# Layer 1 of a four-layer kernel: values stationary, merge and gate by features, three token blocks open in its output projection

## The chip, the cores and the metric

The kernel runs on one core of one Trainium2 chip. The metric is the device time of one execution in microseconds (us). The kernel before takes 2743.85 us, the median of three runs (2741.92 to 2744.84).

## The reference, cut to what matters

Input is x of 512 tokens by 1024 features, in fp32. Two layers of a first block (a mixer with dilated attention, then a mixer with differential attention) are followed by two layers of a second block (a hybrid mixer and a convolutional feed-forward). The change touches only the first layer. What it computes:

```python
proj = h @ w_in                       # h = rmsnorm(x), w_in: 1024 x 10240
q, k = rope(qkv[:, :, 0], pos), rope(qkv[:, :, 1], pos)
v = qkv[:, :, 2]                      # 3 groups x 16 heads x 64
for g, (window, dil) in enumerate(((128, 1), (512, 4), (2048, 16))):
    o, lse = dilated_window_attention(q[g], k[g], v[g], window, dil)
alpha = softmax(stack(lses), axis=0)  # over the three groups, per token and head
o = sum(alpha[..., None] * stack(outs))
y = o.reshape(B, S, 1024) * silu(gate)
h = h + rmsnorm(y @ w_out) * norm_post
```

Only key distances up to `window` in steps of `dil` count, so group 0 is a band of 128 tokens, group 1 works within the four residue classes modulo 4, and group 2 within those of 16.

## The kernel before, in words

**Arithmetic.** Every projection is done in three passes with fp32r operands: an operand is split into a high part (ScalarE, a copy) and a low part (the rest, by GpSimd for weights and VectorE for activations), and hi x hi, hi x lo and lo x hi are summed in PSUM. Attention products and transposes are plain fp32; the profile records an fp32 matmul as two and a transpose as one.

**Order.** One planner (class `Order`) writes a list of steps for all engines; each engine walks the whole list and does its own part of every step, waiting on semaphores, so it is in order on each engine. A `step` appends, `soon(n, f)` runs f after n ticks, and a `tick` comes with half of a group of 12 matmuls with 512 columns (or 24 with 256). `beside(main, side, ratio)` puts `ratio` side steps beside each tick of main work; in layer 1 the main work is the projections and the side work the attention (`R_L1` = 0.8), later the gates with the rest of the attention (`R_G1` = 1.38). SP issues all DMAs, in the order of the list too, and so a wait of SP holds up later weight loads.

**Layer 1.** Heads come in pairs p = 0 to 7 (128 features each), and two of them form one of 4 rounds (`project`). For each p there are four near units (group 0, one block of 128 queries each, tokens in natural order) and four far units (groups 1 and 2 together, tokens sorted by residue modulo 4). A unit has the steps `scores1` (TensorE; VectorE adds the mask and takes the maximum), `exp1` (ScalarE), `turn1` (TensorE transposes the weights, ScalarE copies them out) and `out1` (TensorE, weights stationary with 128 columns, values moving with 64 columns; ScalarE copies the result, 128 tokens x 128 features, out). The near results with their maxima and sums (132 columns) go to DRAM (`near`) and come back in the far order. Then `weigh1` and `merge1` compute the softmax over the groups and add the two results in X, tokens on partitions, in one run of VectorE work.

**Gates.** `token_major` computes each gate tile (256 features) for four token blocks; activations are stationary and weights move with 256 columns. ScalarE takes the tanh, VectorE forms the gate and multiplies X (`times`). Then `chunk` transposes 128 features of X by four TensorE transposes, and ScalarE and VectorE write the high and low parts to AT.

**Output projection.** Four weight tiles l1o0 to l1o3: 0 and 1 hold the first 512 input features for the two halves of the output columns, 2 and 3 the last 512. `by_blocks` does the 4 token blocks one after the other, two PSUM banks each, with the last chunk transposes put between the first groups (`opening`). After a block comes `resid` (ScalarE squares, VectorE reduces, GpSimd takes the power, VectorE scales and adds; ScalarE waits for its end), 2 ticks later `norm u` and 8 ticks later `turn u`, which transposes the block for the next layer with two corner banks (6 and 7) and has ScalarE and VectorE write the high and low parts to UT. The attention's transposes and sums and the chunks use the same two corner banks alternately.

**Lines.** `out1` is L1806 on TensorE, `turn1` L1788, `scores1` L1773 and L1776, `chunk` L1742 (ScalarE L2065), `turn` L1733 (ScalarE L2049), the projections L1669 to L1676. VectorE's `tensor_tensor` calls all have the line L2381; the norm is L2411, the maxima L2483. L1915 is a step of the later layers (`out3`) in which values are stationary.

## Time and profile before

| | |
|---|---|
| median of three runs | 2743.85 us |
| the profiled execution | 2747.37 us |
| its span | 2746.1 us |
| VectorE, ScalarE, GpSimd busy | 44%, 38%, 41% |
| matmul weight loads busy | 79% |
| chain that ended last, TensorE's share | 94% |
| mean granted clock of TensorE | 0.997 |

The span is from the first to the last instruction of the profiled execution. Busy time counts the stretches in which at least one instruction of an engine is under way; matmuls overlap, so a busy TensorE is not one at its peak. Layer 1 runs to about 684 us of the span: rounds of projections and attention to about 555, gates to about 611, then its output projection and the first tile of layer 2.

### The profile page before, as it was taken

The page shows a single profiled execution, that of the slowest core. Times are in us where ns is not written, and L with a number is a line of the kernel's source. Part 1 is how long each engine was busy: PE and PEld are TensorE (multiplying, and loading weights), DVE is VectorE, ACT ScalarE, POOL GpSimd, SP SyncE. Part 2 cuts the span into 40 slices and gives each one's busy share as a digit, 9 for nine tenths or more (in the row PEclk, how much of TensorE's full clock was granted, in tenths as well). Part 3 has the DMA queues.
Part 4 walks back from the last instruction along what each step waited for, and adds up shares of the span by engine and source line. Part 5 has one row for each costly group of instructions (what it writes and reads, how often), then busy time and mean ns, then how long its engine had stood idle before and what let it go on. Part 6 is the DMA issues. An engine that isn't in the chain of part 4 may idle for free.

```text
span 2746.1 us, 36083 instructions
## 1 busy us (share of the span) xinstructions
PE 2696.5 (98%) x13721; PEld 2157.1 (79%) x13721; DVE 1220.5 (44%) x2468; ACT 1051.0 (38%) x2005; POOL 1137.5 (41%) x894
## 2 busy tenths in 40 slices
PE   8999999999999999999999999999999999999998
PEld 6887878898778877776788888887777678888887
DVE  4434343443555356544236424255654423642426
ACT  3333434353345334344333424233435333342422
POOL 4434343424542443333364444444333336444443
PEclk9999999999999999999999999999999999999999
DMA  5424342432422232224253333323222425233321
GB/s 189 135 85 137 95 120 85 136 112 84 123 84 71 75 124 77 77 85 131 84 171 99 108 93 103 96 82 124 77 77 85 131 90 177 88 108 100 100 92 62
DMA packets 215058, 286.40 MB, mean 104 GB/s; under 512 B 16863, under 2 KB 154563, under 8 KB 214117
## 3 DMA queue, kind: packets, MB, share of 16 engines
q1 hardware_dynamic: 214884, 284.08, 33.9%
q8 instruction: 110, 1.80, 0.3%
q14 instruction: 64, 0.52, 0.1%
HBM read 248.31 MB, written 18.94 MB: 97 GB/s over the span
## 4 chain that ended last, share of the span: by engine, by line
PE 94%; DVE 2%; ACT 1%; issue 1%; DMA 1%; POOL 0%; SPq 0%; DVEq 0%; ACTq 0%; POOLq 0%
PE banks L1676 38%; PE banks L1673 29%; PE banks L1669 13%; PE banks L1806 2%; PE banks L1694 2%; PE banks L1733 1%; PE banks L1892 1%; PE banks L1788 1%; PE banks L1709 1%; PE banks L1827 1%; PE banks L1915 1%; PE banks L1965 1%; PE banks L1849 1%; PE banks L1878 1%; PE banks L1773 1%
## 5 line engine op out<-in xcount | busy, mean ns | idle before, releaser
L2979 POOL TENSOR_TENSOR WS<-WR,WS 128x512 fp32r<-128x512 f32 (+2 forms) x676 | 852.1, 1294 | 1061.2 <-ACT WS L2028 1061.2
L1676 PE MATMUL banks<-WS,UT 128*128 128x512 f32 (+1 forms) x3696 | 798.1, 365 | 5.1 <-DVE UT L2381 5.1
L1676 PEld LDWEIGHTS banks<-WS,UT 128*128 128x128 f32 x3696 | 605.6, 190 | 134.9 <-issue 37.3
L1673 PE MATMUL banks<-UT,WS 128*128 128x512 f32 (+1 forms) x2832 | 660.8, 392 | 0.7 <-ACT AR L2210 0.7
L1673 PEld LDWEIGHTS banks<-UT,WS 128*128 128x128 f32 (+1 forms) x2832 | 526.0, 187 | 125.9 <-issue 16.0
L2028 ACT ACTIVATE WS<-WR 128x1024 fp32r<-128x1024 f32 (+1 forms) x344 | 333.1, 1018 | 224.9 <-PE banks L1676 153.6
L1669 PE MATMUL banks<-UT,WS 128*128 128x512 f32 x1536 | 376.4, 399 | 0.0
L1669 PEld LDWEIGHTS banks<-UT,WS 128*128 128x128 f32 x1536 | 285.1, 190 | 65.5 <-issue 6.2
L1676 PE MATMUL banks<-WS,AT 128*128 128x512 f32 x1296 | 308.3, 396 | 0.0
L2977 POOL TENSOR_TENSOR WS<-WR,WS 128x512 fp32r<-128x512 f32 x128 | 180.5, 1442 | 264.9 <-ACT WS L2024 264.9
L1676 PEld LDWEIGHTS banks<-WS,AT 128*128 128x128 f32 x1296 | 242.5, 188 | 58.5 <-ACT WS L2028 0.7
L2381 DVE TENSOR_TENSOR AF<-banks,AF 128x512 f32<-128x512 f32 x128 | 94.2, 787 | 227.3 <-PE banks L1669 227.3
L2914 DVE SCALAR_TENSOR_TENSOR AR<-banks,AR 128x511 f32<-128x511 f32 x84 | 63.0, 750 | 212.4 <-ACT AR L2350 212.4
L2994 POOL TENSOR_TENSOR SM<-SM 128x1 f32<-128x1 f32 (+2 forms) x44 | 47.4, 1077 | 263.7 <-DVE SM L2882 95.4
L2381 DVE TENSOR_TENSOR AR<-AR,banks 128x512 f32<-128x512 f32 x64 | 43.0, 684 | 164.6 <-PE banks L1676 164.6
L2381 DVE TENSOR_TENSOR AR<-AR 128x512 f32<-128x512 f32 (+3 forms) x93 | 98.0, 1053 | 16.3 <-ACT AR L2103 12.9
L2350 ACT ACTIVATE AR<-banks,AR 128x512 f32<-128x512 f32 x84 | 64.9, 773 | 88.4 <-PE banks L1673 80.5
L2483 DVE CUSTOM_DVE_ANT_0 AF<-banks,MF 128x256 f32<-128x256 f32 (+1 forms) x128 | 46.7, 401 | 104.1 <-PE banks L1773 88.0
L1673 PE MATMUL banks<-AT,WS 128*128 128x512 f32 x384 | 88.2, 391 | 0.0
L2024 ACT ACTIVATE WS<-WR 128x512 fp32r<-128x512 f32 x128 | 69.8, 621 | 43.6 <-PE banks L1669 43.6
L1673 PEld LDWEIGHTS banks<-AT,WS 128*128 128x128 f32 x384 | 72.1, 188 | 15.8
L2124 ACT ACTIVATE AF<-banks 128x512 f32<-128x512 f32 (+1 forms) x64 | 36.6, 571 | 111.0 <-PE banks L1788 111.0
(226 smaller groups left out, 2677.6 us busy)
## 6 DMA issues: line engine op xcount, KB each, us to landing
WR<-in_w_in SPq DMA_DIRECT2D x112, 512.0 KB, 3.7
WR<-in_w_up SPq DMA_DIRECT2D x88, 512.0 KB, 3.6
WR<-in_dil_w_in SPq DMA_DIRECT2D x64, 512.0 KB, 3.9
WR<-in_w_down SPq DMA_DIRECT2D x40, 512.0 KB, 3.7
WR<-in_diff_w_in SPq DMA_DIRECT2D x32, 512.0 KB, 3.7
WR<-in_dil_w_in SPq DMA_DIRECT2D x32, 256.0 KB, 3.3
AR<-AF SPq DMA_DIRECT2D x128, 64.0 KB, 2.4
AR<-AF SPq DMA_DIRECT2D x64, 128.0 KB, 2.5
```

Source lines behind the costliest of these rows:

```text
L1669: mm = pe.matmul(B[bank][:, :], slot(i, part)[:, c:c + P], act[:, other, kk, :], start=start, stop=stop)
L1673: mm = pe.matmul(B[bank][0:c, :], w[part][:, kk, g * P:g * P + c], act[:, other, kk, :], start=start, stop=stop)
L1676: mm = pe.matmul(B[bank][:, off:off + n], act[:, other, before_k + kk, g * P:g * P + P], w[part][:, kk, :], start=start, stop=stop)
L1694: mm = pe.matmul(B[c][:, 256 * half:256 * half + 256], w[x][:, kk, (c % 2) * P:(c % 2) * P + P], UT[:, y, kk, 256 * half:256 * half + 256] ...
L1806: mm = pe.matmul(B[ob][:, r:r + 64], fat(7168 + 512 * e + 256 * hh + j * P, P), vj, start=(j == 0), stop=(j == w // P - 1))
L2024: x = se.activation(slot(i, 0)[:, to].rearrange("p (a f c) -> p a f c", f=2, c=32), src, ACT.Copy)
L2028: se.activation(slot(i, 0)[:, v * h:v * h + h], raw(i)[:, v * h:v * h + h], ACT.Copy).then_inc(hi.sem, 1)
L2350: se.activation(d, B[order.bank[i, half][0]][:, :], ACT.Identity, scale=cp[:, 2, f:f + 1], bias=cp[:, 3, f:f + 1]).then_inc(conv_id.sem, 1)
L2381: return ve.tensor_tensor(out_, x, y, op)
L2914: ve.scalar_tensor_tensor(d[:, 1:T], bank[:, 0:T - 1], cp[:, 1, f:f + 1], d[:, 1:T], ALU.mult, ALU.add).then_inc(dve_step, 1)
L2977: ge.tensor_tensor(low, src, high.bitcast(F32), ALU.subtract).then_inc(lo_p.sem, 1)
L2979: ge.tensor_tensor(slot(i, 1)[:, s], raw(i)[:, s], slot(i, 0)[:, s].bitcast(F32), ALU.subtract).then_inc(lo_p.sem, 1)
```

## The change

- `out1`: values are stationary (64 columns) and weights move (128 columns). The two heads of a pair go to the two halves of the output partitions, alternating. Results are by features, 128 features x 128 tokens, in `XT` and `N0`, and no longer go through DRAM. `near` carries only maxima and sums (4 columns).
- `merge1` is replaced by: `share1` (VectorE, the small arithmetic), `rows1` (one TensorE transpose of the 16 share columns, one copy by ScalarE), `send1` (DMA to DRAM), `fetch1` (two DMAs that bring each share row to 64 partitions) and three steps of `merge1` with one VectorE instruction of 128x512 each. They come 2, 5, 7, 9 and 12 to 14 ticks after `weigh1`.
- Gates: `feature_major` with weights stationary and activations moving with 512 columns; `gate1`, `times1` and `parts1` by features; the `chunk` transposes of layer 1 are gone. `R_G1` is 1.7.
- Output projection: `by_three` in place of `by_blocks`.
- The last rotation and spread of the projections come earlier, and the last far units may begin one tick earlier.

```diff
+    def by_three(self, names, finish, parts):
...
+        banks_of = ((0, 1), (4, 5), (2, 3), (0, 1))
+
+        def some(b, j, k0, k1):
+            if len(ws) == j:
+                ws.append(self.open(names[j]))
+            self.bank[ws[j], b] = (banks_of[b][j % 2], 0)
+            self.step("mm", ws[j], b, k0, k1)
+            self.tick(max(1, (k1 - k0) // 2))
+
+        self.fill(i0 + 3)
+        for c in (4, 5, 6):
+            parts(c)
+        for b in range(2):
+            some(b, 0, 0, 4)
+            some(b, 1, 0, 4)
+            if b == 0:
+                self.fill(i0 + 4)
+        for b in range(2):
+            some(b, 2, 0, 2)
+            some(b, 3, 0, 2)
+        some(2, 0, 0, 4)
+        some(2, 1, 0, 4)
+        parts(7)
+        for b in range(2):
+            some(b, 2, 2, 3)
+            some(b, 3, 2, 3)
+        for b in range(2):
+            some(b, 2, 3, 4)
+            some(b, 3, 3, 4)
+            finish(b, ws, banks_of[b])
+        some(2, 2, 0, 4)
+        some(2, 3, 0, 4)
+        finish(2, ws, banks_of[2])
+        for j in range(4):
+            some(3, j, 0, 4)
+            if j < LOOK:
+                self.limit += 1
+                self.split()
+        finish(3, ws, banks_of[3])
...
@@ rotated
+                last = name == "l1k23"
+                self.soon(1 if last else 3, lambda: self.step("rotate", i))
+                self.soon(4 if last else 5, lambda: self.step("spread", i))
...
+    def gates_by_features(self, merged, late):
+        for j in range(4):
+            while j < 3 and 2 * j + 1 not in merged:
+                self.tick()
+                yield 1
+
+            def deal(i, t, j=j):
+                self.step("gate1", i, t)
+                if 2 * j + t not in merged:
+                    late[2 * j + t] = (i, t, j)
+                else:
+                    self.step("times1", i, t, j)
+                    if j < 2:
+                        self.soon(4, lambda: self.step("parts1", 2 * j + t))
+            yield from self.feature_major(f"l1g{j}", deal)
...
@@ layer1
-                    yield
-                    self.step("merge1", p)
-                    merged.add(p)
+                    for due, name in ((2, "share1"), (5, "rows1"), (7, "send1"), (9, "fetch1")):
+                        self.soon(due, lambda name=name: self.step(name, p))
+                    for part in range(3):
+                        self.soon(12 + part, lambda part=part: merge(p, part))
...
@@ tensor, out1
-                    for hh in range(2):
-                        r = 64 * hh
-                        for j in range(w // P):
+                    for j in range(w // P):
+                        for hh in range(2):
+                            r = 64 * hh
...
-                            mm = pe.matmul(B[ob][:, r:r + 64], fat(7168 + 512 * e + 256 * hh + j * P, P), vj,
+                            mm = pe.matmul(B[ob][r:r + 64, 0:P], vj, fat(7168 + 512 * e + 256 * hh + j * P, P),
                                            start=(j == 0), stop=(j == w // P - 1))
...
@@ vector, merge1
+                    if part == 0:
+                        ve.wait_ge(sums_out.sem, sums_out.at["1", l1_last(p, 1)])
+                        ve.wait_ge(rows_in, 32 * (p + 1))
+                        tt(y, y, s0, ALU.mult).then_inc(near_shared.sem, 1)
+                    elif part == 1:
+                        tt(x, x, s1, ALU.mult).then_inc(far_shared.sem, 1)
+                    else:
+                        ve.wait_ge(near_shared.sem, near_shared.at[p])
+                        ve.wait_ge(far_shared.sem, far_shared.at[p])
+                        tt(x, x, y, ALU.add).then_inc(merged.sem, 1)
...
@@ sync
+                elif kind == "send1":
+                    p, = a
+                    sy.wait_ge(rows_out.sem, rows_out.at[p])
+                    if p > 0:
+                        sy.wait_ge(rows_sent, 16 * p)
+                    sy.dma_start(share_rows[p], turned_shares[0:16, :]).then_inc(rows_sent, 16)
+
+                elif kind == "fetch1":
+                    p, = a
+                    sy.wait_ge(rows_sent, 16 * (p + 1))
+                    if p == 7:
+                        sy.wait_ge(summed.sem, summed.at["1", l1_last(5, 1)])
+                    elif p > 0:
+                        sy.wait_ge(merged.sem, merged.at[p - 1])
+                    rows_of = share_rows[p].rearrange("(g r h) l -> h g r l", g=2, h=2)
+                    for h in range(2):
+                        sy.dma_start(shares_of(p)[64 * h:64 * h + 64].rearrange("p g (r l) -> p g r l", r=4),
+                                     rows_of[h].unsqueeze(0).to_broadcast([64, 2, 4, P])).then_inc(rows_in, 16)
```

## Rows read from the trace of the kernel before

**Rows 1.** The page's busy time: us, share of the span, instructions.
```profile
PE 2696.5 (98%) x13721; PEld 2157.1 (79%) x13721; DVE 1220.5 (44%) x2468; ACT 1051.0 (38%) x2005; POOL 1137.5 (41%) x894
```

**Rows 2.** TensorE's waits, 90 to 760 us: total us, times, longest us.
```profile
PE banks L1806 <- ACT AF L2124: 4.9, 7, 0.7
PE banks L1788 <- DVE AT L2381: 1.6, 1, 1.6
PE banks L1773 <- DVE SM L2483: 1.5, 2, 0.7
PE banks L1742 <- DVE AT L2381: 1.2, 1, 1.2
```

**Rows 3.** TensorE's timeline in the gate stage: start us, us, instructions.
```profile
564.42 0.60 PE L1742 MATMUL banks<-CT,AR 128*128 128x128 f32 x4
564.86 0.60 PE L1788 MATMUL banks<-CT,AF 128*128 128x128 f32 x4
...
606.87 4.55 PE L1676 MATMUL banks<-WS,UT 128*128 128x256 f32 x36
611.26 0.60 PE L1742 MATMUL banks<-CT,AR 128*128 128x128 f32 x4
```

**Rows 4.** The chain that ended last, start of layer 2: start us, us.
```profile
684.46 35.36 PE banks L1669 x156
```

**Rows 5.** TensorE's timeline in layer 1, sums with weights stationary.
```profile
129.96 1.65 PE L1676 MATMUL banks<-WS,UT 128*128 128x512 f32 x6
131.45 0.55 PE L1806 MATMUL banks<-AR,AF 128*128 128x64 f32 x4
131.81 1.63 PE L1676 MATMUL banks<-WS,UT 128*128 128x512 f32 x6
...
138.68 1.00 PE L1806 MATMUL banks<-AR,AF 128*128 128x64 f32 x8
139.49 1.64 PE L1676 MATMUL banks<-WS,UT 128*128 128x512 f32 x6
```

**Rows 6.** TensorE's timeline in the hybrid layer, sums with values stationary.
```profile
1100.36 1.66 PE L1676 MATMUL banks<-WS,UT 128*128 128x512 f32 x6
1101.95 0.44 PE L1915 MATMUL banks<-AR 128*64 128x128 f32 x4
1102.32 3.06 PE L1676 MATMUL banks<-WS,UT 128*128 128x512 f32 x12
...
1122.01 0.66 PE L1915 MATMUL banks<-AR 128*64 128x128 f32 x8
1122.59 3.02 PE L1676 MATMUL banks<-WS,UT 128*128 128x512 f32 x12
```

**Rows 7.** DMA issues: queue, count, KB each, median us from issue to landing.
```profile
AR<-in_norm_post SPq DMA_DIRECT2D x2, 512.0 KB, 7.0
```

**Rows 8.** VectorE's timeline, end of a round; in brackets idle us and its releaser.
```profile
487.04 0.17 DVE L2381 TENSOR_TENSOR SM<-AR,SM 128x8 f32<-128x8 f32 x1 [10.62 <-DMA AR<-near]
```

**Rows 9.** TensorE's timeline, output projection of layer 1, from the end of block 0.
```profile
624.12 7.16 PE L1676 MATMUL banks<-WS,AT 128*128 128x512 f32 x30
```

**Rows 10.** VectorE's timeline there: norms (L2411), a turn's low parts, a residual's sum.
```profile
632.38 1.29 DVE L2411 SCALAR_TENSOR_TENSOR AR<-AR,SM 128x1024 f32<-128x1024 f32 x1 [0.73 <-POOL SM L2994]
637.93 1.29 DVE L2381 TENSOR_TENSOR UT<-banks,UT 128x512 fp32r<-128x512 f32 x2 [4.26 <-ACT UT L2049]
...
662.09 1.28 DVE L2411 SCALAR_TENSOR_TENSOR AR<-AR,SM 128x1024 f32<-128x1024 f32 x1 [0.74 <-POOL SM L2994]
...
665.74 1.23 DVE L2381 TENSOR_TENSOR AR<-AR 128x1024 f32<-128x1024 f32 x1
...
669.12 1.28 DVE L2411 SCALAR_TENSOR_TENSOR AR<-AR,SM 128x1024 f32<-128x1024 f32 x1 [0.73 <-POOL SM L2994]
```

**Rows 11.** ScalarE's timeline there: the same turn's high parts.
```profile
637.30 1.09 ACT L2049 ACTIVATE UT<-banks 128x512 fp32r<-128x512 f32 x2 [5.84 <-PE banks L1733]
```

**Rows 12.** A stretch: us, busy us (instructions) by engine, PEclk, DMA share, GB/s.
```profile
344.60:351.40 6.80, 6.80 (x20) 5.74 (x21) 4.04 (x12) 2.58 (x6) 2.71 (x2) 0.50 0.13 48
```

More of the change, by code:

```diff
@@ L429, in by_blocks @@
         self.limit = len(self.tiles)
+    def by_three(self, names, finish, parts):
+        i0 = self.opened
+        self.limit = i0 + 4
+        ws = []
+        banks_of = ((0, 1), (4, 5), (2, 3), (0, 1))
[35 more added lines that the diff above has]
+        finish(3, ws, banks_of[3])
+        self.unit = 0
+        self.limit = len(self.tiles)
     def rotated(self, name):
@@ L549, in project, with merge @@
                 yield from self.rotated(f"l1{name}{p}")
-            self.soon(9, lambda: projected.add((p, 1)))
+            self.soon(8 if p == 3 else 9, lambda: projected.add((p, 1)))
+        def merge(p, part):
+            self.step("merge1", p, part)
+            if part == 2:
+                merged.add(p)
+                if p in late:
+                    self.step("times1", *late.pop(p))
         def attention():
@@ L586, in main @@
                 yield from project(p)
-        late = []
+        late = {}
         att = attention()
         self.beside(main(), att, R_L1)
-        self.beside(self.gates("l1g", lambda j: 2 * j + 1 in merged, late), att, R_G1)
+        self.beside(self.gates_by_features(merged, late), att, R_G1)
         self.lower(self.splits)
         self.drain(att)
+        while 6 not in merged:
+            self.pend.pop(0)[1]()
         self.step("reload", "l1o")
@@ L596, in layer1, with parts @@
         self.lower(self.opened + 1)
-        for x in late:
-            self.step("times", *x)
-        self.by_blocks([f"l1o{j}" for j in range(4)], self.residual("l1o"),
-                       self.opening([("chunk", "l1g", c) for c in range(4, 8)]))
+        def parts(c):
+            while c not in merged:
+                self.pend.pop(0)[1]()
+            self.step("parts1", c)
+        self.by_three([f"l1o{j}" for j in range(4)], self.residual("l1o"), parts)
         self.step("natural_table")
@@ L1097, in build @@
         merged = tally("merged")
+        near_shared = tally("near_shared")
+        far_shared = tally("far_shared")
+        shared = tally("shares")
         gated = tally("gated")
@@ L1272, in build @@
                 weigh_exp.plan(a[0])
+            elif kind == "share1":
+                shared.plan(a[0])
+            elif kind == "rows1":
+                k = takes_corner(("rows", *a))
+                rows_turned.plan(a[0])
+                freed[k] = rows_out.plan(a[0])
+            elif kind == "gate1":
+                i, t = a
+                tanhed.plan((i, t))
+                freed[order.bank[i, t][0]] = gated.plan((i, t))
+            elif kind == "times1":
+                timed.plan((a[0], a[1]))
+            elif kind == "parts1":
+                chunk_hi.plan(("l1g", a[0]))
+                chunk_lo.plan(("l1g", a[0]))
             elif kind == "merge1":
-                merged.plan(a[0])
+                (near_shared, far_shared, merged)[a[1]].plan(a[0])
             elif kind == "gate":
@@ L2140, in scalar @@
                     se.activation(SM[:, QT + 16:QT + 32], SM[:, QT + 16:QT + 32], ACT.Exp).then_inc(weigh_exp.sem, 1)
+                elif kind == "rows1":
+                    p, = a
+                    se.wait_ge(rows_turned.sem, rows_turned.at[p])
+                    if p > 0:
+                        se.wait_ge(rows_sent, 16 * p)
+                    se.activation(turned_shares[0:16, :], B[bank6["rows", p]][0:16, 0:P],
+                                  ACT.Copy).then_inc(rows_out.sem, 1)
+                elif kind == "gate1":
+                    i, t = a
+                    se.wait_ge(proj.sem, proj.at[i, t])
+                    if (i - 1, t) in timed.at:
+                        se.wait_ge(timed.sem, timed.at[i - 1, t])
+                    se.activation(fat(3072 + 512 * t, 512), B[order.bank[i, t][0]][:, :], ACT.Tanh,
+                                  scale=0.5).then_inc(tanhed.sem, 1)
+                elif kind == "parts1":
+                    c, = a
+                    if c == 0:
+                        for name in "qk":
+                            se.wait_ge(*there(index[f"l1{name}23"]))
+                    if c == 4:
+                        se.wait_ge(merged.sem, merged.at[6])
+                    se.wait_ge(timed.sem, timed.at[index[f"l1g{c // 2}"], c % 2])
+                    se.activation(AT[:, 0, c, :].rearrange("p (l r) -> p r l", r=4),
+                                  XT[:, c, :].rearrange("p (r l) -> p r l", r=4), ACT.Copy).then_inc(chunk_hi.sem, 1)
                 elif kind == "gate":
```

115 lines of the change are left out of this document (69 added, 46 removed).

## The prediction

> **What bounds the kernel now.** I read the page's busy line first: TensorE is busy for 98% of the span [rows 1]. So work taken from TensorE shortens the program one for one, and everything else counts only where TensorE has to wait. I then read TensorE's waits from 90 to 760 us, the stretch of layer 1 and the start of layer 2: 4.9 us for ScalarE's copies of transposed weights, 1.6 and 1.2 us for the low parts of chunks, 1.5 us for VectorE's maxima [rows 2]. Waits worth a few microseconds in all can be removed there; the rest has to come from fewer or cheaper TensorE instructions. These are priced from start to start in the timeline, since the durations printed there overlap by some 0.2 us.
>
> **Gates by features.** Removed: 4 tiles x 4 blocks x 24 = 384 matmuls with 256 moving columns. Added: 4 x 2 x 24 = 192 with 512. 36 of the first kind run from 606.87 to 611.26, 0.122 us each [rows 3]; 156 of the second kind take 35.36 us, 0.227 each [rows 4]. 384 x 0.122 = 46.8, 192 x 0.227 = 43.5: **-3.3 us**. Both are shown as they stand, so the bounds are close, -2 and -4.
>
> **Chunk transposes.** The merged values are by features already, so 8 chunks x 4 transposes go. Four last from 564.42 to 564.86, 0.44 us [rows 3]: 8 x 0.44 = **-3.5 us**. With them go two waits: an attention transpose waited 1.6 us for a corner bank (banks 6 and 7, used by turns) that a chunk held, and a chunk 1.2 us for another chunk [rows 2]: **-2.8 us**. The hi/lo split of the chunks stays on ScalarE and VectorE (`parts1`). The split of the last chunk is behind a longer chain than before (shares, a transpose, a DMA out, a DMA in, merge, times), but `by_three` asks for chunk 7 only after four matmul groups of blocks 0 and 1, their half groups with chunks 4 and 5, and two groups of block 2, some 22 us of matmuls.
>
> **Values stationary.** 64 attention units in layer 1; 56 have two weight blocks (8 matmul records, as fp32 is recorded twice) and 8 have one (4 records). Before, one takes 0.81 us (138.68 to 139.49) and 0.36 (131.45 to 131.81) [rows 5]. The new form, values with 64 columns stationary, 128 columns moving, the two heads alternating in the two column halves, is that of L1915 in the later layers: 0.58 us for 8 (1122.01 to 1122.59), 0.37 for 4 (1101.95 to 1102.32) [rows 6]. Its entry costs more: six matmuls of 512 columns ahead of it take 1.59 us (1100.36 to 1101.95) against 1.49 ahead of the old form (129.96 to 131.45), so 0.10 goes on top. 56 x (0.68 - 0.81) = -7.3; 8 x (0.47 - 0.36) = +0.9: **-6.4 us**. Ends: 0 if the new entry costs twice that, and -20 if the pairs overlapped fully (four steps of 0.11, the pace of a transpose with as many columns: 56 x 0.37). I take the middle value because L1915 has the very shapes.
> The trace shows 8 records in 0.68 us against 0.81, a factor of 1.2. The Trainium skill, TensorEngine Tiling (Array Packing), section "Theoretical Speedup", gives up to 2x for a dimension of 64, and its "When to Use Tiling" describes this swap with column tiling. By that factor the 56 units would save 56 x 0.4 = 22 us; L1915's rows don't bear that out here.
>
> **Transposes of shares.** Eight new ones of one instruction (`rows1`), not in this trace. A quarter of a chunk is 0.11 us; a whole chunk's 0.44 is the upper end, 0 the lower: 0 to +3.5, I take 8 x 0.11 = **+0.9 us**, by the instruction count. Small share work (SM tiles) was VectorE's before too.
>
> **VectorE, ScalarE and the queues in the three earlier pairs.** The merge was one run of VectorE work directly ahead of rotations and maxima; now it comes in three steps, 12 to 14 ticks later (a tick is half of a group of 12 matmuls, 1.4 us). TensorE waited 1.5 us for maxima [rows 2]; I take **-1.0 us**. New is a wait of VectorE for the broadcast shares: 512 KB in two DMAs that SP issues at tick 9 while the merge is at 12. A broadcast of 512 KB lands in 7.0 us [rows 7]. Behind the waiting merge stand maxima and ropes. Before, VectorE stood 10.62 us for the `near` transfer at a pair's end [rows 8], and TensorE lost next to nothing there, since the next scores had not begun. Ends: -1.5, and +23 (a rival below).
>
> **Denser attention beside the gates.** R_G1 goes from 1.38 to 1.7, and a gate group is now 12 long matmuls, so 3 or 4 side steps stand in a row instead of 1 or 2: a transpose and the sum that needs its copy more often have little between them. Directly adjacent they cost 4.9/7 = 0.7 us each [rows 2]. Eight units are left for the gate stage; between none and all of them (0 to +5.6) I take three: **+2.0 us**.
>
> **The third block begun: a new wait.** After it, blocks 0 and 1 finish only 6 matmuls apart, and block 2 two groups later. The steps then stand in this order on ScalarE and VectorE: residual 0, norm 0, residual 1, norm 1, residual 2, and only then the hi and lo of turn 0, because a turn comes 8 ticks after its finish; ScalarE also waits for the end of each residual before it goes on. TensorE does turn 0 in time, then one more group, then turn 1, which needs the corner bank that turn 0's low part frees. The chain, from rows: block 0's last matmul ends at 624.12 + 6 x 0.227 = 625.48 [rows 9], its norm at 633.67 [rows 10], so 8.2 us. A norm right behind another takes 670.40 - 663.37 = 7.0 (residual and norm). A residual alone is 666.97 - 663.37 = 3.6 [rows 10]. Then the first half of hi and lo: 637.93 + 0.65 - 637.30 = 1.3 [rows 10, 11]. Sum 20.1 us after block 0's end. TensorE gets to turn 1 after 6 + 48 matmuls (12.3) and turn 0 (8 transposes, 0.9), at 13.2. **+6.9 us.** Before, the only close pair is blocks 2 and 3, with TensorE's next turn further off. Ends: 0 (the rival below) and +9.
> Such a stop also touches the clock. After two stops of 0.7 us the granted clock was at its lower level, 1.2 GHz, from 344.6 to 351.4, with 20 matmuls in 6.8 us [rows 12] where 0.227 each gives 30: 3.4 us lost. After an idle stretch of 6.9 I take a part of that, **+2.0 us** (0 to 3.4).
> The Trainium skill, TensorE: Matmul & The Clock Gate, section "What's actually happening", says that the clock is lowered by default and that activity releases it. By that rule the whole loss of those rows could come back here, 1.4 us more than I charge.
>
> **Sum.** -3.3 - 3.5 - 2.8 - 6.4 + 0.9 - 1.0 + 2.0 + 6.9 + 2.0 = -5.2 us. The profiled execution took 2747.37 us (span 2746.1), so it would take 2742.2; it is 3.5 us above the median of the plain runs, 2743.85, and the difference is carried over to that: **2738.7 us**, 0.19% faster.
>
> **Rivals.**
> No stop at turn 1. If the low part of turn 0 comes out ahead of residual 2 or the residuals run closer together than rows 10 have them, the 6.9 and 2.0 fall away: -14.1, 2729.8 us. For it: turns cost no visible wait in this trace. Against it: the written order. 0.20.
> Cover too thin beside the gates. With 5.6 for the adjacent steps and 3.4 for the clock: -5.2 + 3.6 + 1.4 = -0.2, 2743.7. For it: in-order ScalarE has exponentials, copies, tanh and tile splits to do in the same stretch. Against: maxima and exponentials can run ahead during the 2.7 us of a group. 0.15.
> The shares arrive late, and it is slower. One mechanism: merge part 0 waits for the broadcast, with the maxima of the next unit behind it. 7.0 us to land, less 3 ticks (4.1), leaves 2.9 for each of 8 merges, +23: 2762. It decides once two of those three microseconds reach TensorE, since 8 x 2 - 5.2 is beyond +0.2%. Against it: TensorE hardly felt 10.62 us of such a wait [rows 8]. 0.07.
> Full column overlap: 2738.7 - 14 = 2725. 0.03.
> The forecast itself, with +-4 around it, 2734.5 to 2743: 0.55.
>
> **How the numbers follow.** A measurement of this kernel tells about 0.2% (5.5 us) from no change, so 2738.4 is where "faster" begins, next to my forecast: of its 0.55 I count 0.26 as faster and 0.29 as same. Faster: 0.26 + 0.20 + 0.03 = 0.49. Same: 0.29 + 0.15 = 0.44. Slower: 0.07. The range 2729 to 2747 leaves out the slow rival and full overlap.
>
> **What would show it.** In the changed profile: the sums at 0.58 us from start to start for 8 records; gate matmuls of 512 columns at 0.227; no transposes between gates and the output projection; a wait of nearly 7 us of the turn's transposes for VectorE's UT low part in the output projection of layer 1, and a lower PEclk right after it. VectorE waiting for a DMA ahead of the merges, with TensorE waiting for maxima at the same moment, would make the slow rival right. A turn wait under 2 us would put the result at 2730. I am wrong if TensorE's waits in layer 1 grow at places other than the turn by over 5 us.

## The result and the profile after

The kernel after takes 2747.56 us, the median of 19 runs (2743.89 to 2750.41); the kernel before, on the same chip, 2742.15 (19 runs, 2739.46 to 2744.95). The ratio is 1.0017, 95% interval 1.0010 to 1.0023: a little slower, where 0.19% faster was forecast. The time is just outside the range. The profiled execution took 2747.74 us, its span is 2746.4, that of before 2746.1. So the two traces are 0.3 us apart and the medians 5.4: the profiled execution of before (2747.37 us) was 5.2 us slower than the median of its plain runs, that of after only 0.2. What is read from the two traces below explains the 0.3; the rest is taken up in the part on the prediction.

First the page's busy line, columns as in [rows 1]:

```profile
PE 2682.9 (98%) x13505; PEld 2110.6 (77%) x13505; DVE 1214.8 (44%) x2468; ACT 1050.9 (38%) x2013; POOL 1132.5 (41%) x894
```

TensorE is busy for 13.6 us less, and the span is no shorter: the work has gone and waiting stands in its place. TensorE's waits from 90 to 760 us, total us, times, longest us, against [rows 2]:

```profile
PE banks L1837 <- DVE UT L2518: 6.7, 1, 6.7
PE banks L1910 <- ACT AF L2233: 5.6, 8, 0.7
PE banks L1780 <- POOL WS L3141: 5.1, 2, 3.7
PE banks L1892 <- ACT AF L2223: 4.3, 6, 1.8
PE banks L1880 <- DVE AR L2617: 1.0, 1, 1.0
PE banks L1877 <- DVE SM L2617: 0.5, 1, 0.5
```

(`out1` is now L1910, `turn1` L1892, `scores1` L1877 and L1880, `turn` L1837, the projections L1773 to L1780; ScalarE's copy of turned weights is L2233, its exponentials L2223; GpSimd's low parts of weights are L3141.) In all 23.2 us against 9.2 in [rows 2] (9.8 with two waits under 0.5 us). The first row is the stop that was forecast. The third, TensorE waiting for GpSimd, is not in [rows 2] at all.

Where it happens shows in the starts of two instructions, read from both timelines: the first matmul of the output projection (before 611.62, after 600.89) and the first of l2q0, the tile with which layer 2's query work begins (before 684.30, after 686.84). Up to the first the change gains 10.7 us. Between them it loses 13.3 (72.7 us before, 85.95 after). Behind the second it is 2.2 us shorter, of which up to 1.7 is the clock: before had two stretches of 3.4 us at 1.2 GHz there, after has one.

**The gain.** TensorE's timeline beside the gates; start us, us, instructions, as in [rows 3] and [rows 6]:

```profile
563.65 0.66 PE L1910 MATMUL banks<-AF,AR 128*64 128x128 f32 x8
564.24 0.66 PE L1892 MATMUL banks<-CT,AF 128*128 128x128 f32 x4
...
589.73 8.45 PE L1777 MATMUL banks<-UT,WS 128*128 128x512 f32 x36
598.02 0.27 PE L1919 MATMUL banks<-CT,SM 128*16 128x128 f32 x1
```

Eight records of a sum take 0.59 us from start to start, 36 gate matmuls 8.29, or 0.230 each: both as forecast.

**The loss.** The same view in the output projection, in brackets the wait and what ended it:

```profile
618.29 0.73 PE L1780 MATMUL banks<-WS,AT 128*128 128x512 f32 x2 [3.73 <-POOL WS L3141]
...
653.22 1.94 PE L1837 MATMUL banks<-CT,AR 128*128 128x128 f32 x8 [6.70 <-DVE UT L2518]
...
671.72 3.49 PE L1780 MATMUL banks<-WS,UT 128*128 128x512 f32 x14 [1.38 <-POOL WS L3141]
```

The second of them is the turn of block 1, waiting for the low part of the turn of block 0. The first leads back along the chain of waits (start us, us, what):

```profile
596.60 5.30 DMA AF<-share_rows
601.99 1.11 DVE AR L2518
603.10 0.59 DVE AF L2670
603.69 0.61 DVE AR L2518
604.39 1.09 DVE AR L2518
605.55 1.07 ACT EX L2140
606.69 7.97 POOL EX L3141 x4
614.66 3.59 POOL WS L3141 x2
618.29 14.15 PE banks L1780 x53
```

The shares of pair 6 come back from DRAM, VectorE merges chunk 6, then ScalarE may split tile l1o2, since its high parts go to EX, where pair 6's near result (`N0`) lies until it is merged. GpSimd makes four low parts of l1o2 and only then those of l1o3, for which TensorE stands at 618.29. And GpSimd is slow there, 2.0 us for one low part in the mean (see the last section). During or right after each stop the granted clock falls to its lower level of 1.2 GHz (columns as in [rows 12]; the third number from the end is the clock):

```profile
619.80:623.20 3.40, 3.40 (x10) 2.63 (x8) 2.18 (x2) 1.15 (x1) 2.23 (x2) 0.51 0.42 137
650.50:657.30 6.80, 4.08 (x14) 3.62 (x15) 4.96 (x7) 5.54 (x9) 2.95 (x3) 0.50 0.01 2
657.30:664.10 6.80, 6.80 (x35) 5.64 (x35) 1.52 (x3) 3.12 (x7) 6.17 (x5) 1.00 0.51 153
```

3.40 busy us at half speed lose 1.7, 4.08 lose 2.0.

### The profile page after: what moved, and what is told of

The parts are those of the page before. It is cut to its first block, busy times and chain, and to the rows that moved or that the text cites. A ratio compares the mean times of both kernels' runs of the same rounds, so it can differ in the third digit from the quotient of the medians.

```text
span 2746.4 us, 35721 instructions
## 1 busy us (share of the span) xinstructions
PE 2682.9 (98%) x13505; PEld 2110.6 (77%) x13505; DVE 1214.8 (44%) x2468; ACT 1050.9 (38%) x2013; POOL 1132.5 (41%) x894
## 4 chain that ended last, share of the span: by engine, by line
PE 93%; DVE 3%; ACT 2%; POOL 1%; issue 1%; DMA 0%; SPq 0%; ACTq 0%; DVEq 0%; POOLq 0%
PE banks L1780 36%; PE banks L1777 30%; PE banks L1773 13%; PE banks L1798 2%; PE banks L1910 1%; PE banks L1892 1%; PE banks L1837 1%; PE banks L2003 1%; PE banks L1813 1%; PE banks L2026 1%; PE banks L1938 1%; PE banks L2076 1%; PE banks L1960 1%; PE banks L1989 1%; PE banks L1877 1%
## 5 line engine op out<-in xcount | busy, mean ns | idle before, releaser
L3141 POOL TENSOR_TENSOR WS<-WR,WS 128x512 fp32r<-128x512 f32 (+2 forms) x676 | 854.4, 1295 | 1062.0 <-ACT WS L2140 1062.0
L1780 PE MATMUL banks<-WS,UT 128*128 128x512 f32 (+1 forms) x3312 | 746.1, 374 | 6.9 <-DVE UT L2518 5.5
L1777 PE MATMUL banks<-UT,WS 128*128 128x512 f32 (+1 forms) x3024 | 708.3, 392 | 0.7 <-ACT AR L2347 0.7
L1777 PEld LDWEIGHTS banks<-UT,WS 128*128 128x128 f32 (+1 forms) x3024 | 561.0, 187 | 134.7 <-issue 17.3
L1780 PEld LDWEIGHTS banks<-WS,UT 128*128 128x128 f32 x3312 | 556.8, 189 | 139.5 <-issue 40.2
L1773 PE MATMUL banks<-UT,WS 128*128 128x512 f32 x1536 | 375.7, 398 | 0.0
L1773 PEld LDWEIGHTS banks<-UT,WS 128*128 128x128 f32 x1536 | 283.3, 189 | 69.1 <-issue 10.0
L1780 PE MATMUL banks<-WS,AT 128*128 128x512 f32 x1296 | 309.8, 397 | 3.7 <-POOL WS L3141 3.7
L1780 PEld LDWEIGHTS banks<-WS,AT 128*128 128x128 f32 x1296 | 243.7, 189 | 63.1 <-POOL WS L3141 4.2
L3139 POOL TENSOR_TENSOR WS<-WR,WS 128x512 fp32r<-128x512 f32 x128 | 171.1, 1368 | 266.9 <-ACT WS L2136 266.9
L2518 DVE TENSOR_TENSOR AR<-AR 128x512 f32<-128x512 f32 (+3 forms) x90 | 92.6, 1029 | 16.4 <-ACT AR L2212 12.9
L2233 ACT ACTIVATE AF<-banks 128x512 f32<-128x512 f32 (+1 forms) x64 | 36.4, 569 | 108.1 <-PE banks L1892 107.9
```

The costliest lines, as they stand in the source:

```text
L1773: mm = pe.matmul(B[bank][:, :], slot(i, part)[:, c:c + P], act[:, other, kk, :], start=start, stop=stop)
L1777: mm = pe.matmul(B[bank][0:c, :], w[part][:, kk, g * P:g * P + c], act[:, other, kk, :], start=start, stop=stop)
L1780: mm = pe.matmul(B[bank][:, off:off + n], act[:, other, before_k + kk, g * P:g * P + P], w[part][:, kk, :], start=start, stop=stop)
L2518: return ve.tensor_tensor(out_, x, y, op)
L3139: ge.tensor_tensor(low, src, high.bitcast(F32), ALU.subtract).then_inc(lo_p.sem, 1)
L3141: ge.tensor_tensor(slot(i, 1)[:, s], raw(i)[:, s], slot(i, 0)[:, s].bitcast(F32), ALU.subtract).then_inc(lo_p.sem, 1)
```

## The experiments

Each time is a median. The ratio is to runs of the kernel before on the same chip (their medians lie between 2742.15 and 2743.5), with its 95% interval; kernels that ran on different chips are compared by their ratios (0.0001 is 0.27 us). After has 19 runs, e3 has 8, e10 and e11 have 5, the others 11. "Start" and "to l2q0" are from each trace: the first matmul of the output projection, and the time from it to the first of l2q0.

| kernel | median us | ratio (95%) | start | to l2q0 |
|---|---|---|---|---|
| before | 2743 | 1 | 611.6 | 72.7 |
| after | 2747.56 | 1.0017 (1.0010 to 1.0023) | 600.9 | 85.95 |
| e1_turn_later | 2746.93 | 1.0015 (1.0006 to 1.0024) | 601.2 | 85.5 |
| e2_n0_free | 2743.77 | 1.0003 (0.9994 to 1.0012) | 599.5 | 82.7 |
| e3_blocks | 2749.64 | 1.0025 (1.0015 to 1.0035) | 601.4 | 88.3 |
| e4_both | 2743.04 | 0.9999 (0.9991 to 1.0008) | 601.05 | 81.0 |
| e5_lows_first | 2738.67 | 0.9986 (0.9977 to 0.9994) | 601.0 | 78.3 |
| e6_fast_fill | 2743.55 | 1.0006 (0.9997 to 1.0015) | 598.5 | 83.9 |
| e7_old_spread | 2745.58 | 1.0011 (1.0002 to 1.0020) | 597.15 | 87.5 |
| e8_lows_first_old_spread | 2737.50 | 0.9981 (0.9972 to 0.9990) | 598.7 | 79.3 |
| e9_turn_first | 2744.85 | 1.0008 (0.9999 to 1.0017) | 599.2 | 85.6 |
| e9_turn_first_fill | 2741.40 | 0.9996 (0.9987 to 1.0005) | 595.4 | 85.0 |
| e10_three_alone | 2760.74 | 1.0064 (1.0052 to 1.0077) | 612.8 | 82.4 |
| e11_three_alone_mended | 2752.05 | 1.0037 (1.0025 to 1.0050) | 613.0 | 78.6 |
| e12_lows_first_fill | 2737.78 | 0.9982 (0.9973 to 0.9991) | 595.4 | 80.45 |
| e13_turn1_early | 2740.81 | 0.9989 (0.9980 to 0.9998) | 595.9 | 84.3 |

The starts hold some clock too. Ahead of the output projection, a stretch of 3.4 us at 1.2 GHz (up to 1.7 us lost) lies in the traces of after, e1, e3, e4, e5, e6, e8 and e9_turn_first, one of 6.8 us (3.4 lost) in before, and none in e2, e7, e9_turn_first_fill and e10 to e13.

**e1: the stop at turn 1 taken away.**

```diff
-        finish(2, ws, banks_of[2])
         for j in range(4):
             some(3, j, 0, 4)
+            if j == 1:
+                finish(2, ws, banks_of[2])
-                self.turn_later("u", b, 8)
+                self.turn_later("u", b, 10 if b == 1 else 8)
```

> The changed kernel with two edits in the output projection of layer 1: the residual of block 2 (finish) is put after the second group of block 3 instead of before block 3, and the turn of block 1 comes 10 ticks after its finish instead of 8. Theory A (order): turn 1's 6.7 us stop is made by the high and low parts of turn 0 standing behind residual 2. Then the stop falls under 1 us, the 6.8 us of lowered clock after it go too (3.4 us), and the late weights of the first tile of layer 2 (1.4 us) as well: 9 to 11 us below the changed kernel, 5 to 6 us below the one before. Theory B (shares): the stop only shows that everything here is late because of the merge of p = 6; then the stop moves to another place in the projection and the gain is under 3 us. Theory C (the new attention and gates cost what they save): the gain is as in A, but attention and gates are not shorter than before; the start of the output projection would have to stand at 611 us as before, not 601.

The stop at the turn is gone, and the kernel is as slow. TensorE's waits from 560 us, then GpSimd's timeline (start us, us, in brackets idle us and releaser):

```profile
PE banks L1781 <- POOL WS L3142: 10.8, 2, 7.0
```

```profile
648.38 2.54 POOL L3142 TENSOR_TENSOR WS<-WR,WS 128x512 fp32r<-128x512 f32 x2 [1.18 <-ACT WS L2141]
651.05 0.55 POOL L3157 TENSOR_TENSOR SM<-SM 128x1 f32<-128x1 f32 x1
658.62 0.55 POOL L3157 TENSOR_TENSOR SM<-SM 128x1 f32<-128x1 f32 x1 [7.01 <-DVE SM L2537]
659.13 5.93 POOL L3142 TENSOR_TENSOR WS<-WR,WS 128x512 fp32r<-128x512 f32 x4
```

GpSimd is in order. The power (L3157) of block 2's norm waits 7.0 us for VectorE, and low parts of the first layer 2 tile, ready to be made, stand behind it. One engine's stop was handed to another. Theory A's gain is refuted for this edit; that the stop at turn 1 comes from the order is not.

**e2: pair 6's near result out of EX. e4: both.**

```diff
+        def n0_of(p):
+            return arr(11264, T) if p == 6 else N0[p % 2]
...
-                        se.wait_ge(merged.sem, merged.at[6])
                         se.wait_ge(summed.sem, summed.at["1", l1_last(7, 1)])
```

(and the two users of `N0` take `n0_of(p)`)

> The changed kernel with the near result of p = 6 kept in a region that the third output tile's weights do not overlay, so that their split no longer waits for the merge of p = 6. Theory A and B both: GpSimd's low parts of l1o2 start at about 603 instead of 606.7 us and those of l1o3 at 609.5 instead of 614.6, and the 3.7 us wait of the output projection for them is gone, with 1.7 us of lowered clock behind it: 4 to 5.5 us below the changed kernel; the stop at turn 1 stays at 6.7 us. If the wait came from slow GpSimd instructions (2.0 us each here) and not from their late start, half of it or more stays, and the gain is under 2 us.

> Both edits of the first two kernels together: the residual of block 2 after the second group of block 3 with turn 1 at 10 ticks, and the near result of p = 6 out of the way of the third output tile. Theory A: the gains add, 13 to 16 us below the changed kernel, 8 to 11 us below the one before (0.3 to 0.4% faster). Theory B: no more than the larger of the two, since one wait hides the other.

e2 gains 3.8 us against after (expected 4 to 5.5; the two intervals overlap slightly), with the 6.7 us stop still there (TensorE's waits from 560 us):

```profile
PE banks L1841 <- DVE UT L2521: 6.7, 1, 6.7
PE banks L1784 <- POOL WS L3144: 2.1, 2, 1.4
```

So the late merge of chunk 6, by way of EX and GpSimd's queue, costs about 4 us. e4 isn't told from e2, as theory B has it: the turn's stop becomes GpSimd's 7.0 us, as in e1.

**e3: the order of before, with the merged chunks of after.**

```diff
-        self.by_three([f"l1o{j}" for j in range(4)], self.residual("l1o"), parts)
+        self.by_blocks([f"l1o{j}" for j in range(4)], self.residual("l1o"),
+                       self.opening([(parts, c) for c in range(4, 8)]))
```

> The changed kernel with the old order of the output projection (one block after the other), fed by the new parts. Theory A: no stop at a turn; in its place block 0 asks for chunks 6 and 7 about 8 us after the projection's start, and the shares of p = 7 need until about 615 us, so 3 to 6 us are waited there, and up to 4 us for l1o2's low parts: 2 to 6 us below the changed kernel, so between the same as before and 3 us slower than before to 2 us faster. Theory B: waits for late shares grow to over 10 us, and it is slower than the changed kernel.

2.2 us slower than after by the ratios, which the intervals don't separate. The stop at the turn is gone, and TensorE waits 12.9 us for the parts of the late chunks, as theory B has it:

```profile
614.76 2.90 PE L1781 MATMUL banks<-EX,AT 128*128 128x512 f32 x6 [7.63 <-DVE AT L2519]
...
625.48 2.90 PE L1781 MATMUL banks<-EX,AT 128*128 128x512 f32 x6 [5.26 <-DVE AT L2519]
```

So with the merge by features chunks 6 and 7 come too late for the old order, and going back to it gains nothing. The old order with chunk 6 in a buffer of its own was not run.

**e5: low parts ahead of the norms.** e4, and in block 3:

```diff
             if j < LOOK:
                 self.limit += 1
                 self.split()
             if j == 1:
                 finish(2, ws, banks_of[2])
+            if j < LOOK:
+                self.lower(self.splits - 1)
-                self.turn_later("u", b, 10 if b == 1 else 8)
+                self.turn_later("u", b, (8, 10, 10, 12)[b])
```

> Both edits of e4_both (turn 2 two groups into block 3, merged chunk 6 in a buffer of its own), and after each of the two splits of block 3 the low parts of l2q0- and l2v0- are issued at once, so on GpSimd's in-order queue they stand ahead of the norms' and residual's pow, not behind; turns of the norm come 2 groups later for tokens 1 and 2, 4 later for token 3. Theory A (what is lost is the order on in-order engines): the 7.0 us wait for GpSimd near 650 to 658 and the 1.4 us one at 672 go, and with them 3.4 us of the stretch at the lower clock (half of it lost, 1.7): 7.0 + 1.4 + 1.7 = 10 us below e4_both's 2743.0, 2733 (2730 to 2737), 0.3 to 0.4% faster than before. Theory B (the output projection needs its merged chunks and GpSimd's parts earlier than the gates by features give them, whatever the order): the wait comes again within block 3 or at the first groups of l2q, under 3 us gained, 2740 to 2743.

3.6 us below e4 and faster than before, by 0.14%; A expected 10 and B under 3. GpSimd's part of the waits is down to 0.8 us. What is left is a stop of 3.4 us at 651.8 to 655.3 (TensorE's waits from 600 us, then ScalarE's timeline):

```profile
PE banks L1787 <- DVE UT L2524: 4.5, 3, 3.4
PE banks L1787 <- POOL WS L3147: 0.8, 1, 0.8
PE banks L1787 <- ACT WS L2146: 0.3, 1, 0.3
```

```profile
648.04 0.19 ACT L2310 ACTIVATION_READ_ACCUMULATOR AR<-banks 128x1 f32 x1
653.29 1.08 ACT L2167 ACTIVATE UT<-banks 128x512 fp32r<-128x512 f32 x2 [5.06 <-DVE AR L2524]
```

Block 1 has been transposed since 646, but ScalarE writes its high parts (L2167) only once block 2's residual, ahead of it in its list, has ended on VectorE.

**e6, e7, e8: R_G1, and the three earlier delays.**

```diff
-R0, R1, R2, R3, R_L1, R_L2, R_G1, R_G2 = 0.994, 1.0, 1.45, 0.54, 0.8, 1.2, 1.7, 1.35
+R0, R1, R2, R3, R_L1, R_L2, R_G1, R_G2 = 0.994, 1.0, 1.45, 0.54, 0.8, 1.2, 1.38, 1.35
```

for e6; for e7, and on top of e5 for e8:

```diff
-                self.soon(1 if last else 3, lambda: self.step("rotate", i))
-                self.soon(4 if last else 5, lambda: self.step("spread", i))
+                self.soon(3, lambda: self.step("rotate", i))
+                self.soon(5, lambda: self.step("spread", i))
...
-            self.soon(8 if p == 3 else 9, lambda: projected.add((p, 1)))
+            self.soon(9, lambda: projected.add((p, 1)))
```

> Kernel after with one factor changed, R_G1 1.7 to 1.38: the planner takes a matmul of the gates by features for 19% cheaper, so it puts fewer of them between two steps of attention, and attention of the last tokens is spread over more of the gates. Theory A: the few waits for ScalarE's exps beside the gates (4.3 us before scores' sums, most at 551.7) move by 1 to 2 us either way: 2745 to 2749, nothing that this measurement tells. Theory C (the denser attention beside the shorter gates is what costs): steps stand where they starve less, 3 to 5 us gained: 2743 to 2745.

> Kernel after with the last projection's three delays put back to those of before (the rotation 3 groups later, not 1; the spread 5, not 4; projected 9, not 8). Theory A: this edit buys nothing where the 1.8 us gap at 551.7 stands, since ScalarE's queue decides there, and the delay costs none: 2746 to 2749. Theory C: the earlier rotation is what crowds ScalarE in front of exps 53 and 54; without it the gap of 1.8 us goes: 2745 to 2746.

> e5_lows_first with the three delays of before as in e7_old_spread. Theory A: within 1.5 us of e5_lows_first, so 2731 to 2736. Theory B: as e5_lows_first under B, 2740 to 2743. Theory C: 1.8 us below e5_lows_first.

e6 is 3 us below after, as theory C has it: its output projection starts 2.4 us earlier, and the wait for GpSimd is shorter (1.8 us, not 3.7). e7 starts it 3.7 us earlier, 1.7 of it by the clock stretch that its trace lacks, but is only 1.6 us faster, which is not told from zero. Its wait of 1.8 us beside the gates is down to 1.1, as C expected; in the projection TensorE waits 3.4 us for VectorE's parts of a merged chunk. e8 is 1.2 us below e5, the distance that A allows and not told from zero, though above A's 2731 to 2736. What the old delays gain ahead of the output projection is in good part given back in it.

**e9, with and without e6's factor.** e8 with token block 2 finished after the third group of block 3:

```diff
-            if j == 1:
+            if j == 2:
                 finish(2, ws, banks_of[2])
```

> e8_lows_first_old_spread with token 2 finished one group later (behind the third group of block 3, not the second), so that on ScalarE and VectorE the turned rows of token 1 are written ahead of token 2's residual, not behind it. In e8 TensorE stands 3.4 us at 650 to 654 for that write (ScalarE had it at hand from 646.6, and was held by the residual's end at 653.3). Theory A (the order on in-order engines is what costs): these 3.4 us go, at most 1.5 of them come back as a later turn of token 2, and with the stop goes the 3.4 us at the lower clock (1.7 lost): 2 to 5 us below e8's 2737.5, so 2732.5 to 2735.5. Theory B (the chain of the norms is the limit there): the wait moves to token 2's or 3's turn, 2736 to 2739.

> e9_turn_first with R_G1 1.38 for 1.7, as in e6_fast_fill, which was 4 us below after. If that gain came from the filling beside the gates it adds: 2 to 4 us below e9_turn_first. If it came only by a shorter wait for GpSimd's low parts of l1o3 (1.8 us, not 3.7, in its trace), which the buffer of its own has already removed here: within 1.5 us of e9_turn_first.

Worse than either theory had it: e9_turn_first is 7.4 us above e8. TensorE's waits from 600 us:

```profile
PE banks L1787 <- DVE UT L2524: 6.9, 2, 6.7
PE banks L1844 <- DVE AR L2554: 2.2, 1, 2.2
```

The 3.4 us stop at block 1's rows went, and one of 6.7 came at block 2's, with 10.2 us at the lower clock from within it on. The factor is worth 3.4 us on this kernel, as expected if it adds. The granted clock rises with it, from 0.996 to 0.997 or 0.998 in most runs, and 0.001 of it is up to 2.7 us: how much of the 3.4 is the filling itself isn't shown.

**e10 and e11: the order alone, in the kernel before.** `by_three` of after, and of e5:

```diff
-        self.by_blocks([f"l1o{j}" for j in range(4)], self.residual("l1o"),
-                       self.opening([("chunk", "l1g", c) for c in range(4, 8)]))
+        self.by_three([f"l1o{j}" for j in range(4)], self.residual("l1o"),
+                      lambda c: self.step("chunk", "l1g", c))
```

> Kernel before with the new order of the output projection alone (two token blocks open, the third begun), the chunks being turned by TensorE as before and the gates and values unchanged. Theory A (the order brings the stop at token 0's or 1's turn): the waits of before at that place (2.8 us for the chunks' parts) are traded for a stop of 6 to 8 us and the clock's 1.7 to 3.4: 2747 to 2752, slower than before by 0.2 to 0.35%. Theory B (what costs is that merged chunks come late from the gates by features, and the order only copes with that): with the chunks of before the order costs nothing, 2741 to 2744.

> e10_three_alone with the order of e5_lows_first: token 2 finished two groups later, low parts ahead of the norms, turns later. Theory A: 5 to 8 us below e10, 2741 to 2745; then the gates and values by features are worth the distance to e8_lows_first_old_spread (2737.5), 4 to 8 us. Theory B: within 2 us of e10.

The direction is A's, and the size is twice A's: +17.6 us (0.64%), mended still +10 (0.37%). The mending gives 7.4 us by the ratios, within A's 5 to 8, from a time that A had too low. e10's profiled execution is the fastest of its five runs (2757.49, span 10.1 us above that of before); in it:

```profile
PE banks L1781 <- DVE UT L2429: 6.7, 1, 6.7
PE banks L1790 <- DVE AT L2429: 3.9, 1, 3.9
PE banks L1724 <- POOL WS L3027: 1.3, 1, 1.3
```

The very stop of 6.7 us is there, with none of the other edits. The second row is no part of the changed kernel: chunks 4 to 6 are transposed here ahead of the first matmul, which waits for them, where before puts them between its first groups (1.2 us) and after has no chunk transposes at all. The other four runs are 3 to 5 us above the profiled one. Their granted clock is 0.994 to 0.995 against 0.996, and 0.001 of it is up to 2.8 us, so the clock is enough for that; where it fell isn't on record.

**e12 and e13.** e8 with R_G1 1.38; and that with block 1's turn two groups earlier:

```diff
-                self.turn_later("u", b, (8, 10, 10, 12)[b])
+                self.turn_later("u", b, (8, 8, 10, 12)[b])
```

> e8_lows_first_old_spread with R_G1 1.38 for 1.7. In e9_turn_first_fill this factor let the output projection's first matmul start 3.8 us earlier than in e9_turn_first and was worth 3.4 us in all, on a kernel where GpSimd's low parts were no longer waited for. Theory A: it adds to the order's gain, 3 to 4 us below e8's 2737.5, 2733 to 2735.5. Theory B (the gates by features are at their limit and each gain before the output projection is given back in it as a wait for merged chunks): 2736 to 2738.

> e12_lows_first_fill with the turn of token 1 two groups earlier, before token 2 is finished: ScalarE and VectorE then write token 1's turned rows ahead of token 2's residual, and token 2's norm stands where it stood. Theory A (the place in ScalarE's queue makes the 3.4 us stop at token 1's rows, not the norms' chain): that stop goes, TensorE waits about 1.8 us for the norm of token 1 at its transposes instead, and no new stop comes: 1 to 3 us below e12_lows_first_fill. Theory B (norms' and residuals' chain is the limit, as e9_turn_first suggests, where the wait came again at token 2): the 3.4 us come again at tokens 1, 2 or 3: within 1 us of e12, or slower.

e12 equals e8, as theory B has it: its output projection starts 3.3 us earlier, of which 1.7 is the clock stretch ahead of it in e8's trace, and takes 1.15 us longer. e13 is 3.0 us above e12, some 2 by the ratios. TensorE's waits from 600 us:

```profile
PE banks L1787 <- DVE UT L2524: 3.8, 2, 3.6
PE banks L1787 <- DVE AT L2524: 2.5, 2, 1.5
PE banks L1844 <- DVE UT L2524: 2.4, 1, 2.4
```

The 3.6 us stop is at block 2's rows now (from 662.6), beside a wait of 2.4 at the earlier turn. So theory B fits this last piece: with blocks finished this close together, the chain residual, norm, turn of each block, some 7 us, is the limit. In the two other places tried in ScalarE's list (e9, e13) only the block changed at which TensorE stands.

e8 and e12 are the fastest, 0.9981 (0.9972 to 0.9990) and 0.9982 of before. Their granted clock is that of before, 0.998 in the mean, so the 5 us are not the clock's.

## Why the prediction was wrong, by its steps

**Gates by features, chunk transposes: right.** 0.230 us a matmul where 0.227 stood. The `chunk` transposes and their waits are gone.

**Values stationary: right in mechanism, under-sized.** The eight records take 0.59 us, and in sum over the 480 records TensorE goes from 53.4 to 39.1 us from start to next start, -14.3; the matmul ahead of a sum takes 5.3 us more in all (18.4 to 23.6 over 64 of them), which holds the longer waits for ScalarE's copies. Net -9.0 against -6.4: the records give 14.3 where 12.8 stood, and the entry takes 5.3 where 6.4 stood. Eight records go from 0.83 to 0.59 us, a factor of 1.4, far from full overlap; the 1.2 of the prediction had the entry in it.

**Waits beside the gates: over the +2.0.** From 90 to 600 us TensorE waits 11.4 us where it waited 7.9. That is +3.5 for the terms that I had at -1.6 (a chunk's corner bank), -1.0 and +2.0. e6 confirms that denser side work is part of it. Up to the output projection the two errors nearly cancel: -11.6 forecast (without the transposes of three chunks and the wait that lie behind its first matmul), -10.7 measured, 1.7 of it from the clock (3.4 us at the lower level there, not 6.8 as in [rows 12]). About 1 us is left open.

**The third block begun: the step that failed.** The text had +6.9 for the stop and +2.0 for the clock, against the transposes of three chunks and a wait, -2.5, in the same stretch: +6.4. Measured: +13.3. The stop itself came where and as large as forecast, 6.70 against 6.9, for the reason given: from block 0's end (632.97) to TensorE going on (653.22) it is 20.2 us where 20.1 stood, and e1 removes the stop. Three things were not in the sum. First, the sentence that chunk 7 has 22 us of cover looked at the wrong chunk: what was late was chunk 6, since the weight split into EX waits for it, with GpSimd's low parts of two tiles behind that: 3.7 us (e2: 3.8 us back). Second, low parts behind a norm's power in GpSimd's order, 1.4 us in after and 7 in e1 and e4 (e5 leaves 0.8). Third, the clock: 1.7 + 2.0 = 3.7 us, not 2.0. Together 5.1 - 0.2 + 1.7 = 6.6 of the missing 6.9. The prediction's own sign of being wrong came with them: TensorE's waits outside the turn grew by 23.2 - 6.7 - 9.2 = 7.3 us (6.7 with the two short ones of before), over its 5.

**From the profiled execution to the plain runs: a second step that failed.** The prediction took 3.5 us off, the distance of before's profiled execution from its median, and carried it over to after. After's profiled execution is 0.2 us from its median. So of the 8.9 us between 2738.7 and 2747.56, 5.5 are the trace's (2742.2 against 2747.74) and 3.3 this step's. The granted clock goes with it. The profiled execution of before has 0.997, with three stretches, 13.6 us in all, at 1.2 GHz ahead of its last 2 us. Of the 30 runs of before beside e1, 15 have 0.999 (mean 2741.3 us), 7 have 0.998 (2743.5) and 8 have 0.997 (2745.2). Of the 19 of after, 11 have 0.997 (2746.3) and 8 have 0.996 (2748.4). At 0.997 the two kernels are about 1 us apart; by estimate the other 4 of the 5.4 us come with a lower clock in after. Its profiled execution has 10.2 us of lowered clock at the stops of the output projection, where before has none; that they are what lowers the clock in the plain runs too is likely, and not shown.

**The whole, by runs.** The order costs 17.6 us in the kernel before (e10), where I had 8.9. That is not its price in after: 3.9 us of it are the wait for chunks that after doesn't have, against 1.2 in before, and e10's runs have a granted clock 0.0036 lower in the mean than before's, by estimate 7 us at what the runs of before lose per 0.001 (2 us) and up to 10 if TensorE is busy throughout. The 8.9 had 2.0 for the clock. If the parts of the change simply added, the rest of it would gain 1.0064 - 1.0017 = 0.0047, 12.9 us, and with the mended order 1.0037 - 0.9986 = 0.0051, 14 us, where the other terms make -14.1. With waits that only e10 and e11 have, this closeness is partly luck. No run has values stationary or gates by features alone. Shown are the under-sized price of the order, in the rows of the output projection, and that the old order gains nothing in its place (e3).

**The rivals.** No stop at turn 1: false, 6.70 us. Late shares: the mechanism was real, but not at the maxima where I had put it, and at 4 us instead of 23. Cover too thin beside the gates: waits there grew by 3.5 us, about as far as that rival had it, but the loss that decided lay behind them. I gave slower 0.07; a queue in which a late DMA's wait passes from VectorE to ScalarE to GpSimd deserved more.

## What to carry to other kernels

Where engines are in order, price a new order of work by each engine's own list: for every step that is moved ahead, ask which step of another block now stands in front of it, on GpSimd too, and which of the waits in that list ends last. A late transfer is dangerous through what shares its buffer: follow every semaphore that a buffer's reuse needs, not only the reader of the data. Removing one stop in such a chain often shows the next of the same length; run the removal before believing the gain.

## What the runs showed of the hardware

GpSimd and VectorE hold each other up when both read SBUF. GpSimd's and VectorE's timelines in the kernel after (the third row of GpSimd is one of the four of the second):

```profile
592.81 5.03 POOL L3141 TENSOR_TENSOR WS<-WR,WS 128x512 fp32r<-128x512 f32 x4 [14.21 <-ACT WS L2140]
606.69 7.97 POOL L3141 TENSOR_TENSOR EX<-WR,EX 128x512 fp32r<-128x512 f32 x4 [8.85 <-ACT EX L2140]
609.19 4.22 POOL L3141 TENSOR_TENSOR EX<-WR,EX 128x512 fp32r<-128x512 f32 x1
```

```profile
604.39 1.07 DVE L2518 TENSOR_TENSOR AR<-AR 128x512 f32<-128x512 f32 x1
...
608.61 3.65 DVE L2518 TENSOR_TENSOR AT<-AR,AT 128x512 fp32r<-128x512 f32 x3 [2.35 <-ACT AT L2276]
...
615.42 1.70 DVE L2518 TENSOR_TENSOR AR<-AR 128x512 f32<-128x512 f32 x1
```

A low part takes 1.26 us with VectorE nearly idle. The 2.0 us at 606.69 are a mean: three of the four took 1.3 us and one 4.2. Beside that one VectorE made the three low parts of a chunk, from two SBUF inputs each, the last two in 1.1 us: GpSimd stood and VectorE hardly slowed. From 614 us on both are slow: low parts take 1.7 to 2.1 us, and an addition of the merge 1.70 where one with GpSimd idle takes 1.07. DMA traffic is not the cause. In this trace 308 of GpSimd's 128x512 instructions have no VectorE instruction beside them and all took 1.26 to 1.32 us, a tenth of them with the DMA engines over 0.9 busy. The Trainium skill, SBUF — State Buffer, section "Who interferes with whom", says that a VectorE instruction with two SBUF inputs contends with a GpSimd instruction that reads SBUF, because they share a read port; the trace agrees. What the page says of the other side being fully blocked it says of VectorE's 2-port modes; here the row of 4.2 us looks like that, and the rows behind it show both sides 1.3 to 1.7 times as long.

The six low parts from 606.69 to 618.25 take 4.0 us longer than six at 1.26, so without the slowing the 3.7 us stop would by estimate be gone too. In e2 they are slow as well (1.8 us in the mean before the projection needs them), and the earlier start alone is enough.

The clock fell to 1.2 GHz with stops of 3.7 and 6.7 us, and in e5 with one of 3.4, each time for 3.4 to 10.2 us; in after it fell within the 6.7 us stop (at 650.5, the stop lasts from 646.5 to 653.2) and 1.5 us behind the 3.7 us one. A stop of 6.7 us thus cost 8.7 in after; in e2 the same stop lay in 10.2 us of low clock with 5.78 of them busy:

```profile
643.40:653.60 10.20, 5.78 (x18) 4.93 (x19) 6.65 (x9) 6.88 (x10) 4.87 (x5) 0.50 0.01 2
```

Half of the busy time is lost, 2.9, and the stop costs 9.6.
